# Exponent rows in three bfloat16 parts, and eight modulation chunks computed in the mLSTM's steps: a two-layer hybrid kernel on one core

## The reference, cut to what matters

```python
m = (silu(cvec) @ w_mod + b_mod)      # w_mod: 1024 x 6144 per layer
sh_m, sc_m, g_m, sh_f, sc_f, g_f = split(m, 6)
```

```python
Lm = exp(a_cs[t] - a_cs[s])                       # SSD
W  = exp(b[t] - b[s] + ig[s] - m_star[t]) * (q @ k.T)   # mLSTM
```

## Time and profile before

| | |
|---|---|
| median of 3 executions | 1364.68 us (1362.76 to 1365.07) |
| profiled execution | 1374.02 us, of which the span of its instructions is 1372.2 us |
| busy in the profiled execution | PE 1157.2, PEld 615.8, DVE 510.4, ACT 248.8, POOL 214.1 us |
| mean granted TensorE clock | 0.889 of 2.4 GHz |
| read from HBM | 308.40 MB |

### The profile page before, as it was taken

How to read it: one execution, slowest core, us unless ns; L and a number is a source line. 1 busy time by engine, 2 the same in 40 slices (tenths; PEclk the granted TensorE clock), 3 DMA queues, 4 the chain that set the end, 5 groups by cost and what they waited for, 6 DMA issues and landing times.

```text
span 1372.2 us, 13712 instructions
## 1 busy us (share of the span) xinstructions
PE 1157.2 (84%) x5189; PEld 615.8 (45%) x5189; DVE 510.4 (37%) x1034; ACT 248.8 (18%) x476; POOL 214.1 (16%) x206
## 2 busy tenths in 40 slices
PE   3999979799897499999994499998977569879992
PEld 1445445444443344444452254456644345434441
DVE  1433637545501622222222675325352343223112
ACT  2231211365402300000012322110001201100001
POOL 0000022000011163222112200000000065422001
PEclk8899959999998699999998699995557879999997
DMA  9532326679062179999998031140006339999982
GB/s 343 207 117 69 110 80 239 245 274 395 14 268 91 74 261 416 414 415 394 350 421 327 2 123 61 62 152 33 0 0 251 147 145 408 412 418 419 423 339 106
DMA packets 74366, 309.78 MB, mean 226 GB/s; under 512 B 11789, under 2 KB 14013, under 8 KB 57131
## 3 DMA queue, kind: packets, MB, share of 16 engines
q1 hardware_dynamic: 63083, 286.39, 53.5%
q0 software_dynamic: 10336, 19.06, 3.8%
q10 hardware_dynamic: 864, 3.15, 0.6%
HBM read 308.40 MB, written 15.34 MB: 236 GB/s over the span
## 4 chain that ended last, share of the span: by engine, by line
PE 71%; DMA 10%; DVE 9%; ACT 3%; issue 3%; SPq 2%; POOL 1%; POOLq 0%; DVEq 0%
PE psum L1774 9%; PE psum L1777 8%; DMA arena<-in_moe_w 8%; PE psum L1145 7%; PE psum L1054 6%; PE psum L1809 5%; PE psum L537 5%; PE psum L1804 4%; PE psum L529 3%; PE psum L373 2%; PE psum L1158 2%; PE psum L1384 2%; PE psum L1385 2%; PE psum L510 1%; SPq L1969 1%
## 5 line engine op out<-in xcount | busy, mean ns | idle before, releaser
L1890 POOL DMA_INDIRECT arena<-hdram,idxl x128 | 128.6, 1005 | 268.4 <-DVE arena L1849 173.0
L1864 DVE TENSOR_TENSOR arena<-arena,psum 128x512 f32<-128x512 f32 x32 | 22.0, 688 | 275.1 <-PE psum L1774 145.1
L1145 PE MATMUL psum<-arena,ring 128*128 128x512 f32 (+1 forms) x256 | 97.8, 539 | 0.0
L1078 POOL TENSOR_TENSOR xres<-xres,arena 128x512 f32<-128x512 f32 x12 | 15.2, 1264 | 488.3 <-DVE arena L1067 488.3
L1774 PE MATMUL psum<-arena 128*64 128x256 f32 x736 | 84.5, 386 | 6.8 <-DMA arena<-in_moe_w 5.6
L1774 PE MATMUL psum<-ring,arena 128*64 128x256 f32 x672 | 78.0, 390 | 13.2 <-DVE arena L1849 9.2
L1777 PE MATMUL psum<-ring,arena 128*128 128x512 f32 x176 | 79.8, 611 | 10.1 <-DVE arena L1849 9.3
L1054 PE MATMUL psum<-ring,arena 128*128 128x512 f32 x192 | 84.7, 603 | 1.5 <-ACT arena L1039 1.5
L1849 DVE STREAM_TRANSPOSE arena<-arena 128x1024 f32<-128x1024 f32 x32 | 64.9, 2030 | 17.3 <-DMA arena<-hdram,idxl 17.3
L1832 ACT ACTIVATE arena<-psum 128x512 f32<-128x512 f32 x32 | 19.1, 597 | 282.4 <-PE psum L1804 174.0
L1774 PEld LDWEIGHTS psum<-arena 128*64 128x64 f32 x736 | 54.3, 139 | 33.0 <-DMA arena<-in_moe_w 6.9
(11 more groups left out here) (369 smaller groups left out, 1660.8 us busy)
## 6 DMA issues: line engine op xcount, KB each, us to landing
ring<-in_moe_w SPq DMA_DIRECT2D x48, 2048.0 KB, 14.8
arena<-in_moe_w SPq DMA_DIRECT2D x48, 2048.0 KB, 15.0
ring<-in_w_mod SPq DMA_DIRECT2D x24, 2048.0 KB, 9.1
ring<-in_od_w_in SPq DMA_DIRECT2D x6, 2048.0 KB, 8.9
ring<-in_ev_w_in SPq DMA_DIRECT2D x3, 2048.0 KB, 9.6
arena<-ydram POOLq DMA_DIRECT2D x6, 1024.0 KB, 7.1
ring<-in_ev_w_out SPq DMA_DIRECT2D x2, 2048.0 KB, 12.2
ring<-in_od_w_out SPq DMA_DIRECT2D x2, 2048.0 KB, 7.8
```

Of the source, the lines that this page charges most:

```text
L1145: mm = pe.matmul(bank(bk, tok.stop - tok.start), w[:, k, P * (b % 4):P * (b % 4) + P], hT[:, k, tok], start=k == 0, stop=k == KD - 1)
L1890: pool.indirect_dma_start(xq[e % NX][:, 256 * g:256 * g + 256], None, xrows(l), bass.IndirectOffsetOnAxis(ap=idxl[:, g, e:e + 1], axis=0), ...
```

## The change: what it does

**Exponents.** A float32 row x is written as the sum of three bfloat16 rows: a = bf16(x), b = bf16(x - a), and bf16(x - a - b). DVE makes a and b, and GpSimd lays the three parts of each direction under one another, at partitions 0, 32 and 64 (72 rows, the rest zero). A new constant `headsel` (72 x 8, bfloat16) has ones where the partition modulo 32 is the head. Its column, against the 72 rows, adds the three parts in PSUM. So the four matmuls of L778 and L1361 and the eight of L1351 have bfloat16 operands. PE waits for GpSimd's part before the first step.

**Modulation.** The first 16 chunks (LATE = 16) are computed where they were, with three of them left in the attention, at heads 9, 19 and 29. Layer 1's last eight (g_m, sh_f, sc_f, g_f) are loaded behind layer 1's input weights and computed one in each mLSTM step, with bank 7 for the transposes too. So `pe_mod_rows` of such a chunk waits until DVE has read the chunk before it.

```diff
+PARTS = 2 * DIR1 + H
+    headsel = cb[0:PARTS, 2560 + 6 * NT:2560 + 6 * NT + H]
+    LATE = MODC + 4
-    before0 += [mod_src(*m) for m in MODS[FIRST:]]
+    before0 += [mod_src(*m) for m in MODS[FIRST:LATE]]
     before1 = [cols(od, OD_GATES, OD_GATES + 32)] + [cols(od, 512 * i, 512 * i + 512) for i in range(6)]
+    before1 += [mod_src(*m) for m in MODS[LATE:]]
     def pe_mod_rows(m):
+        if m >= LATE:
+            pe.wait_ge(*pe_more("mcol_done"))
         weights_here(mod_pos(m))
+    def mod_bank(m):
+        return 6 if m < LATE else 7
     def pe_mod_cols(m):
         pe.wait_ge(*pe_more("modrow_ready"))
-        if m > 0:
+        if 0 < m < LATE:
             pe.wait_ge(*pe_more("mcol_done"))
+    def dve_split(x, a, b, rest):
+        dve_step(dve.tensor_copy(a[0:ROWS], x))
+        dve_step(dve.tensor_tensor(rest[0:ROWS], x, a[0:ROWS], ALU.subtract))
+        dve_step(dve.tensor_copy(b[0:ROWS], rest[0:ROWS]))
+    def pool_split(i, a, b, rest, parts):
+        pool.wait_ge(S("dg_ready"), 2 * i + 1)
+        for d in range(2):
+            pool_step(pool.memset(parts[d][0:PARTS], 0.0))
+        for d in range(2):
+            src = slice(DIR1 * d, DIR1 * d + H)
+            pool_step(pool.tensor_copy(parts[d][0:H], a[src]))
+            pool_step(pool.tensor_copy(parts[d][DIR1:ROWS], b[src]))
+            last = pool.tensor_tensor(parts[d][2 * DIR1:PARTS], rest[src], b[src], ALU.subtract)
...
-    ATT_LEFT = 2 * MODC - OUT_MOD - 1
+    ATT_LEFT = LATE - OUT_MOD - 1
     def pe_ssd():
         pe.wait_ge(S("ssd_prepared"), 1)
+        pe.wait_ge(S("dg_ready"), 2)
...
-                    mm = pe.matmul(psum[:, g, P * h:P * h + P], ident[0:ROWS, r:r + 1].broadcast_to([ROWS, P]),
-                                   tq[0:ROWS, 0, P * t:P * t + P], start=False, stop=h == 3)
+                    mm = pe.matmul(psum[:, g, P * h:P * h + P], headsel[:, r:r + 1].broadcast_to([PARTS, P]),
+                                   ssd_parts[d][0:PARTS, P * t:P * t + P], start=False, stop=h == 3)
...
     def pe_ml():     # the matmuls of decays(n) likewise, with ml_parts
         for i, (st, d) in enumerate(SSD_ITER):
             if st >= 2:
                 if n == 0:
                     decays(1)
+                pe_mod_rows(LATE + i)
                 ...   # numerator, decays(n + 2)
+            else:
+                pe_mod_rows(LATE + i)
             if st < 3:
                 ...   # state product
+            pe_mod_cols(LATE + i)
     def dve_ml():
...
+            dve_mod(LATE + i)
     def act_ml():    # the exponentials where they were, and behind them in each of 8 steps:
+            act_mod(LATE + i)
...
             dve_ml_out(OUT_ORDER[1])
+            dve_mod_bias(1, LATE - MODC, MODC)
+            dve_acol(1, 1)
             dve_out(LAT, 1)
```

More of the change, by code:

```diff
@@ L650, in dve_true_order, with halfview @@
         dve.wait_ge(*dve_more("tq_ready"))
+    def dve_split(x, a, b, rest):
[11 more added lines that the diff above has]
+            last = pool.tensor_tensor(parts[d][2 * DIR1:PARTS], rest[src], b[src], ALU.subtract)
+            last.then_inc(S("pool_step" if d == 0 else "dg_ready"), 1)
+            if d == 0:
+                pool.wait_ge(*pool_more("pool_step"))
+        pool.wait_ge(S("dg_ready"), 2 * i + 2)
+    def halfview(at, n):
+        return view(at, [n // 2]).bitcast(BF16)
+    SSD_SPLIT = (halfview(19968, TOK), halfview(20224, TOK), view(20480, [TOK]))
+    ssd_parts = [halfview(24704 + 256 * d, TOK) for d in range(2)]
     TOT = stat[0:ROWS, 8:12]
@@ L670, in dve_ssd_rows @@
         dve_true_order(tq, sq, 4)
+        dve_split(rows(tq, 0), *SSD_SPLIT)
         dve.tensor_tensor(dg[0:ROWS, :, :], ETOT.unsqueeze(2).broadcast_to([ROWS, 4, ROWS]),
@@ L1281, in dve_od_rows_end @@
         dve_true_order(tqo, sqo, 5)
+        a, b, rest = (v.rearrange("p (q n) -> p q n", q=2) for v in ML_SPLIT)
+        dve_split(tqo[0:ROWS, 2:5:2, STREAM:TOK], a, b, rest)
         dve.tensor_tensor(dgo[0:ROWS, :, :], SPA[:, 0:3].unsqueeze(2).broadcast_to([ROWS, 3, ROWS]),
@@ L1473, in act_ml @@
     def act_ml():
-        for i in range(4):
-            for g in range(2):
-                act.wait_ge(*act_more("arg_ready"))
-                act.activation(wto[i % 2][g], wto[i % 2][g], ACT.Exp).then_inc(S("exp_ready"), 1)
+        for i in range(8):
+            if i == 0 or i >= 4:
+                n = 0 if i == 0 else i - 3
+                if n < 4:
+                    for g in range(2):
+                        act.wait_ge(*act_more("arg_ready"))
+                        act.activation(wto[n % 2][g], wto[n % 2][g], ACT.Exp).then_inc(S("exp_ready"), 1)
+            act_mod(LATE + i)
     OUT_ORDER = [1, 0]
@@ L1922, in hybrid_program @@
     used += [("in_full", n) for n in (4, 7, 11, 15, 19)]
-    used += [("mod_full", i + 1) for i in range(FIRST, 2 * MODC)]
+    used += [("mod_full", i + 1) for i in range(FIRST, LATE)]
     used += [("out_full", 4), ("out_full", 8)]
@@ L1939, in hybrid_program @@
     used += [("in_full", EVEN_FILLS + n) for n in (2, 6, 10, 14, 18, 20, 22)]
+    used += [("mod_full", i + 1) for i in range(LATE, 2 * MODC)]
     used += [("out_full", 10), ("out_full", 12)]
@@ L2146, in _ @@
             pool_zero(0)
+            pool_split(0, *SSD_SPLIT, ssd_parts)
             pool_ssd()
@@ L2154, in _ @@
             pool_zero(1)
+            pool_split(1, *(v.rearrange("p (q n) -> p q n", q=2) for v in ML_SPLIT), ml_parts)
             pool_out(LAT)
@@ L2227, in _ @@
             dve_mod_bias(0, FIRST, MODC)
-            dve_mod_bias(1, 0, MODC)
-            for l, which in ((0, 1), (1, 0), (1, 1)):
-                dve_acol(l, which)
+            dve_mod_bias(1, 0, LATE - MODC)
+            dve_acol(0, 1)
+            dve_acol(1, 0)
             dve_out(ALL, 0)
@@ L2263, in _ @@
             pe_grow(0, 0, (0, 1))
[L2264 removed]
+            pe_out(ALL, 5 + LATE)
             pe_norm(ALL)
@@ L2308, in constants @@
     f[:, 601] = np.arange(P) // 64 - 4
-    b = np.zeros((P, 2560 + 6 * NT), np.float32)
+    b = np.zeros((P, 2560 + 6 * NT + H), np.float32)
+    b[:, 2560 + 6 * NT:] = np.arange(P)[:, None] % DIR1 == np.arange(H)
     b[:, 2432:2560] = np.arange(P)
```

34 lines of the change are left out of this document (19 added, 15 removed).

## The result

| | before | changed |
|---|---|---|
| median, lowest to highest (18 runs each) | 1365.2 us (1362.0 to 1377.2) | 1355.5 us (1352.1 to 1359.9) |
| profiled execution, its span | 1374.0, 1372.2 us | 1352.6, 1350.8 us |
| mean granted clock there | 0.889 | 0.901 |

The change makes the kernel about 1% faster: ratio 0.9906, 95% interval 0.9888 to 0.9924. This ratio is the recorded one of fast runs against fast runs; it is not the quotient of the two medians, which is 0.9929. The forecast was 1348, with 1333 to 1371 as its range.

A forecast was written before the change was run, and what follows sets the result against it. PE was taken to bound early SSD steps, attention and the mLSTM numerator; the MoEs only shift. SSD -0.7, attention -5 and mLSTM -11 sum to -17 from 1364.7, giving 1348 us, range 1333 to 1371.

The forecast's parts named there:

- two rivals: Inside the range: chunks were cover for the clock (1362) and moved chunks eat the mLSTM's gain (1359), chance 0.15 each.
- Price of a group: Four bfloat16 exponent matmuls instead of eight float32 records: saves 1.4 us at the low, 0.8 at the full clock.
- SSD, -0.7: SSD stage: gross -7.2 us from cheaper exponents, +6.5 for a falling clock; bounds -9 and +11.
- The clock's price of +6.5: SSD: PE's longer waits lower the clock; 1.1 us per step taken for six steps.
- Attention, -5: Attention with eight of eleven chunks gone: -11.5 us at full clock, +6.5 for the clock; bounds -12 and +4.
- gross of -11.5: Attention at the full clock: removing all eleven chunks saves 18.3 us, the three remaining cost +6.8.
- The clock's share, +6.5: Attention: without the chunks PE is less busy, the clock may fall and context and latent groups lengthen; +6.5 us taken.
- rival 3: The chunks were cover for the clock: SSD +5, attention +3, mLSTM -11, in all -3, 1362 us; chance 0.15.
- mLSTM, exponents -16: mLSTM: four `decays` on the path, some 3.5 us saved with the first, 4.2 with the others, if the clock stays low.
- Chunks: mLSTM, one moved chunk per step: new wait on DVE, clock partly raised; stage -11 us taken, between +17 and -25.
- the low case: mLSTM all at the low clock: numerators of 11.6 us, the last ending at 1044 against 1027.3, +17.
- Covered work and transfers, 0: Splits on DVE and GpSimd lie beneath other work, and moved chunk loads delay nothing: 0 us, both MoEs keep their length.

The follow-up runs named there:

- e1: Only the bfloat16 exponents in SSD and mLSTM, all 24 chunks where they were before, against the kernel before: 1351.0 us, ratio 0.9880.
- e9: Changed kernel plus unread dense matmuls in attention, two after each of the first six heads, one after each later head without a chunk: ratio 0.9842.
- e12: bfloat16 exponents in the mLSTM only, the SSD's exponents as float32 rows, chunks where they were before: ratio 0.9903 to the kernel before.
- e6: bfloat16 exponents alone, chunks where they were before, with the SSD's chunk transposes moved behind the diagonal product: ratio 0.9868 to the kernel before.
- e4: Changed kernel with the SSD's four transposes of a chunk and their reduce behind the step's diagonal product: ratio 0.9868 to the kernel before.
- e7: e6 plus 117 dense matmuls whose result nobody reads (covers), in PE's waits in the SSD and mLSTM: 1327.6 us, ratio 0.9716.
- e11: e7 plus one more cover after each of the first seven heads inside each of the mLSTM's first three numerators: ratio 0.9792.

## Why the prediction was right, and where its steps were off

The forecast of 1348 was 7.5 us low, the changed kernel's time within its range and the sign right. The range spans 38 us and takes in two rivals, so that it held says little of the mechanism; and part of it is luck, since the SSD was forecast 5 us too dear and the attention 5 us too cheap, and these cancel. Sum by stages: forecast -0.7, -5, -11; over the profiles that share code, SSD -6 (83.1, three with float32 rows, against 77.1, six with parts), attention 0 (94.7, three with the chunks and the order of before, against 94.2, the changed kernel and its repeat), mLSTM -8.8 (in both profiles). With the 2 us that come back behind the mLSTM (below) that is -17, and the medians give -10, the ratio of 0.9906 -13. The stage lengths are of single executions, and that of before lay 9 us above its median, so they overstate what came from before; how the 4 to 7 us divide over the stages stays open.

**Price of a group.** Forecast 1.4 and 0.8 us saved. Measured from start to start at the full clock 0.23 us for the four matmuls, so 0.86 saved of 1.09; at the low one 0.42, so 1.58 saved of 2.00:

```profile
180.01 0.63 PE L819 MATMUL psum<-arena,cb 72*128 72x128 bf16 x4
180.43 0.63 PE L816 MATMUL psum<-cb 128*128 128x512 bf16 x1
```

The group's weight loads, over the SSD by line and form, and in the timeline at the full clock:

```profile
L819 PEld LDWEIGHTS psum<-arena,cb 72*128 72x128 bf16 x64 | 5.7, 109 | 6.9 <-issue 5.6
209.40 0.21 PEld L819 LDWEIGHTS psum<-arena,cb 72*128 72x128 bf16 x3 [0.21 <-issue]
```

The Trainium skill's page "TensorE: Matmul & The Clock Gate" (section "LDWEIGHTS") has a load time by its columns, from which 107 ns is estimated for 128. One record takes about that here, 109 ns in the mean. But the records overlap, three of them in 0.21 us, so four loads set no floor of 0.43 us at the full clock, and the trace doesn't bear out the smaller saving of 0.65.

**SSD, -0.7.** The wait grew as foretold (to 1.93 us, 2.4 forecast), and so did steps 2 to 5: 9.5 each before, 10.3 to 11.0 after, 4.3 together. Steps 6 and 7 gave back 0.3 and 1.2 (0.8 each forecast). The clock's price of +6.5 for six steps was thus 2 us too high in this profile, and right in e1's (5.5 more in steps 2 to 5, 0.8 less in the last two). The larger miss is the start. With float32 rows steps 0 and 1 take 26 to 29 us and the clock rises at 194 to 203; with parts they take 17 to 19 and it rises at 180 to 185. I had counted 5.6 us of saved matmuls there and no earlier rise. The term was mis-sized; the lower bound of -9 held for the mean of -6, while the first profile alone has -9.3.

**Attention, -5.** The gross of -11.5 was about right: with the clock held (e9) the stage is 10 us shorter. The clock's share, +6.5, was too small: it took all of it. This is rival 3's mechanism, and it was right for this stage: the eight chunks were cover. Its price was not (+3, measured 0), and its other part, SSD +5, was wrong.

**mLSTM, exponents -16** at the low clock: measured -14.8 (e1, e12, e6: 97.0 to 97.3 against 111.8). **Chunks:** the steps are as worked out for the full clock (5.38 us, forecast 5.5), the rows ahead of the last three numerators ran low as foretold, three numerators a little better than 7.5 to 8.5 (6.75, 7.07, 6.75), the fourth as the low case had it (11.7). Total -8.8 for -11. L382 stood behind L411 as foretold.

But the step that put exponents and chunks into one sum hid what e1 shows: without the chunks the stage is 6 us shorter still, at the lower clock. By the forecast's own terms (-16 for the exponents, -11 for both) the move cost 5 in the mLSTM and earned 5 in the attention. Measured, it earns nothing in the attention and costs 6 in the mLSTM. Behind it, up to the MoE, the changed kernel takes 2 us less than the one before and 3 less than e1; its clock is up again 4 us behind the stage's end (at 1025), that of e1 10 us behind (at 1031). That the whole change is slower than its exponents alone is likely from the stages and not shown by the ratios (e1 against the changed kernel 0.3 to 0.5% in favour of e1, e6 against e4 equal).

**Covered work and transfers, 0.** Outside the three stages the profile differs from that of before by 0.2 us ahead of the SSD, -1.4 between the SSD and the attention, 0.7 from there to the mLSTM and -2 behind it; both MoEs keep their length to 0.2 us.

The best kernel run is e7: exponents in parts, chunks between the heads as before, transposes behind the diagonal product, covers in the SSD and the mLSTM, 0.9716 (0.9698 to 0.9735). Whether e9's 10 us in the attention can be had on top of it, by covers there and the chunks in a free place elsewhere, wasn't tried.

## What to carry to other kernels

Work taken from PE turned into time here only where PE's wait behind it didn't grow instead and where the clock stayed up: look at the granted clock of the stretch, and at what the removed work did for it, before counting microseconds. Work moved into a stage whose clock is down can raise it and pay for itself, but whether it does hangs on what stands around it: the same move gained 8 us and lost 6 in two pairs of kernels that differ in the exponents alone, so test it in the kernel that it is for. A few dense bfloat16 matmuls of no use in PE's waits are a quick test of a clock theory. Here they also gained 1.5% on top of the bfloat16 exponents (0.9868 to 0.9716), but 0.8% with float32 ones.

## What was not expected of the hardware

- PE can be busy without a gap at 1.2 GHz and stay there: attention heads with 64-row scores for 14 of 14 us (in the changed kernel, above), numerators of 64-row and 129-column matmuls for 11.6 us. With one or two more 128-row, 512-column bfloat16 matmuls in each head without a chunk, at 0.22 us each, the clock stayed at 2.4 GHz through those heads (e9).
- The clock can fall in the middle of a numerator in which PE has no wait, with covers between its heads (e11, above) and without them (e7, timeline of PE):

```profile
925.56 0.49 PE L1438 MATMUL psum<-arena 64*128 64x129 f32 x2
925.97 0.60 PE L1437 MATMUL psum<-arena 128*128 128x129 f32 x2
926.50 0.79 PE L1438 MATMUL psum<-arena 64*128 64x129 f32 x2
```

- In the changed kernel's profile four bfloat16 matmuls of 128 columns, each with new weights, took 0.23 us together at 2.4 GHz, though one load's record is 0.109 us in the mean: the loads' records overlap (above).
